# Gate and up biases of the routed experts: loaded once as rows and added by a matmul that picks two of them

## The chip, the cores and the metric

The kernel runs on one core of one Trainium2 chip. The metric is the device time of one execution in microseconds (us). Three runs of the kernel before took 3603.2, 3605.3 and 3605.53 us (median 3605.3 us). All data are fp32.

## The reference

One decoder layer over 256 tokens of width 2048: a token mixer (a diagonal state-space branch and a chunked delta-rule branch, merged by gates), a layer norm, a layer of routed experts, and a second layer norm. The change lies in the routed experts. Each token goes to 4 of 32 experts, and an expert computes, on the tokens that it was given:

```python
gate = jnp.minimum(xb @ w_gate[e] + b_gate[e], SWIGLU_LIMIT)
up = jnp.clip(xb @ w_up[e] + b_up[e], -SWIGLU_LIMIT, SWIGLU_LIMIT)
h = gate * jax.nn.sigmoid(SWIGLU_ALPHA * gate) * (up + 1.0)
return h @ w_down[e] + b_down[e]
```

with `w_gate[e]` and `w_up[e]` of 2048 x 512, `w_down[e]` of 512 x 2048, `b_gate[e]` and `b_up[e]` of 512, and `SWIGLU_LIMIT` 7. The results are summed per token with the router's weights (`b_down` is added elsewhere, by one matmul with the weights of all experts).

## The kernel before

The program is written by hand per engine, with semaphores; the order on each engine is the order of the code. SyncE (SP) issues all DMAs. The phases run one after the other: the projections and the two branches, the gating, the output projection, a layer norm, the router, the routed experts (from about 2547 us to 3571 us in the profiled execution), and the last layer norm.

The experts run as 16 pairs (`PAIRS`), each expert with room for 64 tokens (`CAP`), so that a pair fills 128 partitions or 128 columns: partitions 0 to 63 of a bank belong to the first expert of the pair and 64 to 127 to the second. Where an expert had more than 64 tokens, a flag sends all engines into another branch (`over > 0`), which this input doesn't take. Per pair `i`, TensorE (PE) does, in `sparse(i)`:

- `sgate(i)` (through `expand`, the matmuls of L860): 32 calls of `mm` into bank 0, alternately for the left and the right expert, each with 64 columns of the array and 512 moving columns; each call is two MATMUL records in the profile.
- `sup(i)` (L860 too): the same into bank 1. Gate and up together are the 128 records of L860 in a pair.
- `gather(i + 1)` (L849): selects the tokens of the next pair by a matmul with a 0/1 matrix `Psel`.
- `scatter(i - 1, 0, 6)` and `(6, 8)` (L907; 8 calls, 16 records): spreads the results of the pair before back over the tokens. Between them `turn_hidden` (L876), behind them `turn_weights` (L881), both transposes.
- `sdown(i)` (L891): the down projection, 64 records, again with 64 columns of the array each.

`mm` with start=True begins a sum in a bank, and the later calls add to it. The full array (128 columns) is used in L849, L876, L881 and L907, half columns in L860 and L891.

VectorE (DVE) does `select(i)` (L1592: builds `Psel`, four instructions), `stake_gate(i)` (L1600: reads bank 0, adds the bias tile `pbrow[:, 0]`; L1602: the minimum), `stake_up(i)` (L1608: reads bank 1, adds `pbrow[:, 1]`; L1611: the weights `Pw` for the scatter; L1616: minimum and maximum; L1618, L1621: the products) and `add_scatter` (L1629: adds a bank to the sum of the layer). ScalarE (ACT) copies banks to the tiles that PE reads next (L1119, L1127, L1129, L1137) and does the sigmoid (L1123).

The weights pass through six buffers (`unit`), each of 2 MB: 12 loads per pair (four quarters each of gate, up and down), issued by `reload_unit` (L350), which waits until PE has read the buffer (`unit_read`). The biases of a pair are loaded by `load_biases(i)` (L361): four DMAs, each of which reads one row of 512 numbers and writes it to 64 partitions. From pair 1 on they stand between the second and the third load of weights, behind a wait on `brow_free`, which `stake_up(i - 1)` sets when it has read the bias tile. `stake_gate(i)` waits for them.

The tile `masks` has 8 x 128 columns. Columns 128 to 1023 hold masks of the delta-rule branch and later a copy of state inputs; the experts don't use them. `ident` is a 128 x 128 identity.

Of the kernel before, what the change touches and what calls it, by code (L numbers as in the profile page):

```python
# [67 lines left out]
def build(nc, x, w_in, conv_w, a_log, dt_bias, norm_w, w_dn, lam_re, lam_im, log_dt, b_re, b_im, c_re, c_im,  # L68
# [3 lines left out]
    with ExitStack() as ctx:  # L72
# [138 lines left out]
        ysb = at(4096, D)  # L211
        pbrow = at(6144, 2, F_E)
        Psel = at(TM + 768, MT, 2, CAP)
# [53 lines left out]
        unit_read = [sem(f"unit{i}_free") for i in range(UNITS)]  # L267
        brow_free = sem("brow_free")
        gate_done, gate_taken, up_done, up_taken = sem("gate_done"), sem("gate_taken"), sem("up_done"), sem("up_taken")
# [17 lines left out]
        def _(sp):  # L287
# [69 lines left out]

            def load_biases(i):
                for o in range(2):
                    for c, b in enumerate((b_gate, b_up)):  # L360
                        sp.dma_start(pbrow[CAP * o:CAP * o + CAP, c],  # L361
                                     b[ds(2 * i + o, 1)].rearrange("o n -> (o n)").partition_broadcast(CAP)).then_inc(brow_loaded, 16)

# [28 lines left out]
            load_unit(UNITS - 1, 0)  # L392
            load_biases(0)
            sp.dma_start(ln2row[:, 0], ln2_g.partition_broadcast(P)).then_inc(ln2_loaded, 16)
# [3 lines left out]
            with sp.If(over < 1):  # L398
                for j in range(UNITS, PER_PAIR):
                    reload_unit(j, 0)  # L400
                with sp.Fori(1, PAIRS) as i:
                    for j in range(PER_PAIR):
                        if j == 2:
                            sp.wait_ge(brow_free, i)
                            load_biases(i)
                        reload_unit(j, i)
            with sp.If(over > 0):
                for j in range(UNITS):
                    sp.wait_ge(unit_loaded[j], 16)
                sp.wait_ge(brow_loaded, 64)  # L410
                load_gate(0)
                load_up(0)
                with sp.Fori(0, N_E - 1) as e:
                    sp.wait_ge(gate_done, e + 1)
                    sp.sem_inc(load_free, 1)
                    load_gate(e + 1)
                    sp.wait_ge(dn_taken[1], 4 * e + 1)
                    sp.sem_inc(load_free, 1)
                    load_down(e)
                    sp.wait_ge(up_taken, 2 * e + 2)  # L420
                    sp.sem_inc(load_free, 1)
                    load_up(e + 1)
                sp.wait_ge(dn_taken[1], 4 * N_E - 3)
                load_down(N_E - 1)
# [95 lines left out]
        def _(pe):  # L520
# [332 lines left out]
            def expand(bank, first, i):  # L853
                for q in range(4):
                    j = first + q
                    pe.wait_ge(unit_loaded[j % UNITS], 32 * i + 16 * (j // UNITS) + 16)
                    w = unit[j % UNITS].rearrange("p o (k n) -> p o k n", k=4)
                    for k in range(4):
                        for o in range(2):
                            last = mm(ps[bank][CAP * o:CAP * o + CAP, :], xg[:, 4 * q + k, CAP * o:CAP * o + CAP], w[:, o, k],  # L860
                                      start=q == 0 and k == 0, stop=q == 3 and k == 3)
                    last.then_inc(unit_read[j % UNITS], 1)

            def sgate(i):
                pe.wait_ge(xg_taken, 4 * i + 4)
                if not isinstance(i, int) or i > 1:
                    pe.wait_ge(sc_taken, 8 * i - 8)
                expand(0, 0, i)

# [298 lines left out]
        def _(dve):  # L1168
# [383 lines left out]
            def take_gate(e):  # L1552
                dve.wait_ge(gate_done, e + 1)
                dve.wait_ge(brow_loaded, 32 * e + 96)
                for m in range(MT):
# [33 lines left out]
            def select(i):  # L1589
                for m in range(MT):  # L1590
                    for o in range(2):
                        V.tensor_scalar(Psel[:, m, o], slots1, column(pos, m, i, o), column(sel, m, i, o),  # L1592
                                        ALU.is_equal, ALU.mult)
                dve.drain()  # L1594
                dve.sem_inc(p_built, 1)

            def stake_gate(i):
                dve.wait_ge(unit_read[3], 2 * i + 1)
                dve.wait_ge(brow_loaded, 64 * i + 64)
                V.tensor_tensor(sgb, ps[0][:, :], pbrow[:, 0], ALU.add)  # L1600
                dve.drain()
                V.tensor_scalar(sgb, sgb, LIMIT, None, ALU.min)  # L1602
                dve.drain()
                dve.sem_inc(gate_taken, 1)

            def stake_up(i):
                dve.wait_ge(unit_read[1], 2 * i + 2)
                V.tensor_tensor(shb, ps[1][:, :], pbrow[:, 1], ALU.add)  # L1608
                for m in range(MT):
# [4 lines left out]
                dve.sem_inc(up_taken, 1)  # L1614
                dve.sem_inc(brow_free, 1)
                V.tensor_scalar(shb, shb, LIMIT, -LIMIT, ALU.min, ALU.max)  # L1616
                dve.drain()
                V.scalar_tensor_tensor(out=shb, in0=shb, scalar=1.0, in1=sgb, op0=ALU.add, op1=ALU.mult)  # L1618
# [67 lines left out]
```

## Time and profile before

| what | value |
|---|---|
| median of three runs | 3605.3 us (3603.2 to 3605.53) |
| the profiled execution | 3604.39 us, of which span 3602.3 us |
| PE busy | 3206.1 us, 89% of the span |
| PE weight loads | 2437.7 us, 68% (they overlap the matmuls) |
| DVE busy | 1047.1 us, 29% |
| ACT busy | 482.2 us, 13% |
| DMA moved | 660.87 MB, mean 183 GB/s |
| chain of waits, share of the span | PE 60%, issue 16%, DVE 9%, DVE's sequencer 5%, DMA 3% |

All times of the trace count from the span's start. PE's matmuls are pipelined, their ends are modelled, and a record's duration (592 ns for 512 moving columns at full clock) is longer than the distance from one to the next: distances between starts, or the length of a whole run of records, tell what a matmul costs. In the chain of waits each piece ends where the next begins.

### The profile page before, as it was taken

How to read it: one execution, taken by the hardware profiler on the slowest of the kernel's cores; microseconds unless marked ns; L12 is line 12 of the kernel's file. 1: busy time of each engine (PE TensorE's matmuls, PEld its weight loads, DVE VectorE, ACT ScalarE, POOL GpSimd, SP SyncE). 2: the span in 40 equal slices, each digit the busy share in tenths (PEclk: the TensorE clock that was granted, in tenths of full speed). 3: DMA queues.
4: the chain of work that ended last, by engine and by line, in shares of the span. 5: the costliest groups of instructions: out<-in, count | busy, mean ns of one | idle time of the engine just before them, and what ended most of it. 6: DMA issues, size and time to landing. Idle time of an engine off the chain costs nothing.

```text
span 3602.3 us, 44020 instructions
## 1 busy us (share of the span) xinstructions
PE 3206.1 (89%) x17395; PEld 2437.7 (68%) x17395; DVE 1047.1 (29%) x2650; ACT 482.2 (13%) x632; POOL 106.8 (3%) x189
## 2 busy tenths in 40 slices
PE   6999999999997868787788787895899999999996
PEld 6988888888886757676676676685545445454542
DVE  1433433433423026465570000003111111121114
ACT  1121121121121021101100000000011101111111
POOL 1010010010010000000000000000000000000000
PEclk9999999999999888798898998897899999999998
DMA  5232232242230622232223334273499999999995
GB/s 148 71 116 93 70 116 70 80 130 70 70 116 9 178 94 94 68 99 83 80 94 117 97 113 140 87 275 117 192 406 410 396 409 396 410 409 396 409 396 212
DMA packets 325973, 660.87 MB, mean 183 GB/s; under 512 B 41840, under 2 KB 271344, under 8 KB 275440
## 3 DMA queue, kind: packets, MB, share of 16 engines
q1 hardware_dynamic: 325904, 659.85, 49.9%
q8 instruction: 56, 0.92, 0.1%
q14 instruction: 13, 0.11, 0.0%
HBM read 657.73 MB, written 2.10 MB: 183 GB/s over the span
## 4 chain that ended last, share of the span: by engine, by line
PE 60%; issue 16%; DVE 9%; DVEq 5%; DMA 3%; ACT 2%; SPq 1%; ACTq 1%; POOL 1%; POOLq 1%
PE bank L553 17%; PE bank L860 12%; PE bank L849 6%; PE bank L891 6%; PE bank L907 3%; PE bank L618 3%; PE bank L616 3%; PE bank L762 2%; DVE arena L1401 2%; DVE arena L1403 2%; PE bank L609 2%; DVEq L1400 2%; DMA arena<-in_w_glu_a_dram 2%; PE bank L734 1%; PE bank L703 1%
## 5 line engine op out<-in xcount | busy, mean ns | idle before, releaser
L553 PE MATMUL bank<-arena 128*128 128x256 f32 x5632 | 1285.1, 387 | 117.3 <-DMA arena<-in_w_glu_a_dram 71.0
L553 PEld LDWEIGHTS bank<-arena 128*128 128x128 f32 x5632 | 1081.0, 195 | 274.3 <-issue 90.4
L860 PE MATMUL bank<-arena 128*64 128x512 f32 x2048 | 442.2, 592 | 0.7 <-ACT arena L1119 0.7
L860 PEld LDWEIGHTS bank<-arena 128*64 128x64 f32 x2048 | 147.1, 137 | 292.5 <-issue 290.5
L721 PE MATMUL bank<-arena 128*128 128x256 f32 x1024 | 229.1, 387 | 19.9 <-DMA arena<-in_w_dn_out_dram 19.9
L849 PEld LDWEIGHTS bank<-arena 128*128 128x128 f32 x1024 | 224.8, 311 | 15.4 <-issue 12.2
L721 PEld LDWEIGHTS bank<-arena 128*128 128x128 f32 x1024 | 198.8, 195 | 49.5 <-DMA arena<-in_w_dn_out_dram 16.0
L849 PE MATMUL bank<-arena 128*128 128x128 f32 x1024 | 227.8, 384 | 3.1 <-DVEq L1594 3.1
L891 PE MATMUL bank<-arena 128*64 128x512 f32 x1024 | 223.3, 594 | 7.7 <-ACT arena L1129 7.7
L891 PEld LDWEIGHTS bank<-arena 128*64 128x64 f32 x1024 | 72.2, 137 | 148.4 <-issue 137.0
L1629 DVE TENSOR_TENSOR arena<-arena,bank 128x512 f32<-128x512 f32 x128 | 87.7, 687 | 198.6 <-PE bank L907 198.5
L1600 DVE TENSOR_TENSOR arena<-bank,arena 128x512 f32<-128x512 f32 x16 | 11.1, 692 | 458.6 <-PE bank L860 458.6
L609 PE MATMUL bank<-arena 128*128 128x128 f32 x896 | 123.9, 281 | 7.8 <-DVEq L1253 3.9
L762 PE MATMUL bank<-arena 128*128 128x256 f32 x512 | 115.4, 390 | 12.6 <-DMA arena<-in_w_mix_out_dram 12.6
L609 PEld LDWEIGHTS bank<-arena 128*128 128x128 f32 x896 | 112.4, 191 | 21.0 <-DVEq L1266 13.1
L1435 DVE TENSOR_TENSOR arena<-arena,bank 128x512 f32<-128x512 f32 x8 | 5.5, 689 | 413.9 <-ACTq L1086 413.9
L762 PEld LDWEIGHTS bank<-arena 128*128 128x128 f32 x512 | 100.3, 196 | 27.7 <-issue 13.3
L618 PE MATMUL bank<-arena 128*128 128x128 f32 x896 | 118.3, 275 | 0.0
L616 PE MATMUL bank<-arena 128*128 128x128 f32 x896 | 118.2, 275 | 0.0
L907 PE MATMUL bank<-arena 128*128 128x512 f32 x256 | 115.2, 593 | 2.5 <-DVEq L1613 1.8
L1262 DVE TENSOR_TENSOR arena<-arena,bank 128x512 f32<-128x512 f32 x112 | 77.1, 688 | 137.7 <-PE bank L618 137.7
L616 PEld LDWEIGHTS bank<-arena 128*128 128x128 f32 x896 | 113.3, 192 | 2.9
(277 smaller groups left out, 2264.7 us busy)
## 6 DMA issues: line engine op xcount, KB each, us to landing
arena<-in_w_in_dram SPq DMA_DIRECT2D x72, 2048.0 KB, 8.4
arena<-in_w_gate_dram SPq DMA_DIRECT2D x64, 2048.0 KB, 16.3
arena<-in_w_up_dram SPq DMA_DIRECT2D x64, 2048.0 KB, 13.3
arena<-in_w_down_dram SPq DMA_DIRECT2D x64, 2048.0 KB, 19.2
arena<-in_w_dn_out_dram SPq DMA_DIRECT2D x16, 2048.0 KB, 11.3
arena<-in_w_glu_a_dram SPq DMA_DIRECT2D x8, 2048.0 KB, 8.3
arena<-in_w_glu_b_dram SPq DMA_DIRECT2D x8, 2048.0 KB, 13.7
arena<-in_w_mix_out_dram SPq DMA_DIRECT2D x8, 2048.0 KB, 11.1
```

What stands on the lines that cost most here:

```text
L553: last = mm(ps[bank][:, ct * T:ct * T + T], ring[:, buf, k, ct * P:ct * P + P], rhs[:, k, :], start=k == 0, stop=k == KD - 1)
L609: last = mm(ps[3 + 2 * c][:, a * P:a * P + P], At[:, c, a], Ti[:, c, a], start=True, stop=True)
L616: mm(ps[3 + 2 * c][:, a * P:a * P + P], Tt[:, c, a], Pm[:, c, a], start=True, stop=True)
L618: last = mm(ps[4 + 2 * c][:, a * P:a * P + P], Pm[:, c, a], Tt[:, c, a], start=True, stop=True)
L721: last = mm(ps[1][:, ct * T:ct * T + T], ring[:, buf, k, ct * P:ct * P + P], oT[:, half * KD + k, :], start=half == 0 and ct == 0 and k == ...
L762: last = mm(ps[bank][:, m * SC:m * SC + SC], mg[:, k, m * P:m * P + P], ring[:, buf, k, :], start=k == 0, stop=k == KD - 1)
L849: last = mm(ps[4 + b][:, k * P:k * P + P], h1[:, m, 4 * b + k::KD], Psel[:, m].rearrange("p o c -> p (o c)"), start=m == 0, stop=m == MT - 1)
L860: last = mm(ps[bank][CAP * o:CAP * o + CAP, :], xg[:, 4 * q + k, CAP * o:CAP * o + CAP], w[:, o, k], start=q == 0 and k == 0, stop=q == 3 ...
L891: last = mm(ps[4 + n][CAP * o:CAP * o + CAP, :], shT[:, k, CAP * o:CAP * o + CAP], unit[j % UNITS][:, o, n * 512:n * 512 + 512], start=k = ...
L907: last = mm(ps[(2, 3, 0, 1)[n % 4]][:, :], pwT[:, (n // 4) * P:(n // 4) * P + P], ysb[:, (n % 4) * 512:(n % 4) * 512 + 512], start=True, s ...
L1262: V.tensor_tensor(Ti[:, c], Ti[:, c], ps[3 + 2 * c][:, :].rearrange("p (a t) -> p a t", a=GV), ALU.subtract)
L1629: V.tensor_tensor(av, av, ps[(2, 3, 0, 1)[n % 4]][:, :], ALU.add).then_inc(sc_taken, 1)
```

## The change

The two bias arrays (32 experts x 512 numbers each) are loaded once, as they are: expert `e` on partition `e`, gate in `bias_gu[:, 0]`, up in `bias_gu[:, 1]`. `select(i)` builds beside `Psel` a 32 x 128 matrix `pair_pick`: column `c` of the left half has its one on row `2i`, of the right half on row `2i + 1`. At the head of `sgate(i)` two matmuls with `pair_pick` stationary and the bias rows moving (32 rows, all 128 columns of the array, 512 moving columns) begin the sums in banks 0 and 1 with the biases on every partition; the matmuls of `expand` then all add. The four DMAs per pair, the wait on `brow_free` and DVE's waits for the biases go. On DVE the addition of the bias goes out of L1600 and L1608, and what stood behind each of them (minimum; minimum and maximum) reads the bank directly, so that L1602 and L1616 go; one copy into `pair_pick` is added in `select`.

```diff
-        pbrow = at(6144, 2, F_E)
+        bias_gu = at(6144, 2, F_E)
+        pair_pick = masks[0:N_E, P:2 * P]
...
-            def load_biases(i):
-                for o in range(2):
-                    for c, b in enumerate((b_gate, b_up)):
-                        sp.dma_start(pbrow[CAP * o:CAP * o + CAP, c],
-                                     b[ds(2 * i + o, 1)].rearrange("o n -> (o n)").partition_broadcast(CAP)).then_inc(brow_loaded, 16)
+            def load_biases():
+                for c, b in enumerate((b_gate, b_up)):
+                    sp.dma_start(bias_gu[0:N_E, c], b).then_inc(brow_loaded, 16)
...
-            load_biases(0)
+            load_biases()
...
                     for j in range(PER_PAIR):
-                        if j == 2:
-                            sp.wait_ge(brow_free, i)
-                            load_biases(i)
                         reload_unit(j, i)
...
                             last = mm(ps[bank][CAP * o:CAP * o + CAP, :], xg[:, 4 * q + k, CAP * o:CAP * o + CAP], w[:, o, k],
-                                      start=q == 0 and k == 0, stop=q == 3 and k == 3)
+                                      start=False, stop=q == 3 and k == 3, skip_group_check=True)
...
             def sgate(i):
                 pe.wait_ge(xg_taken, 4 * i + 4)
+                if isinstance(i, int) and i == 0:
+                    pe.wait_ge(brow_loaded, 32)
                 if not isinstance(i, int) or i > 1:
                     pe.wait_ge(sc_taken, 8 * i - 8)
+                for c in range(2):
+                    mm(ps[c][:, :], pair_pick, bias_gu[0:N_E, c], start=True, stop=False, skip_group_check=True)
                 expand(0, 0, i)
...
+                V.tensor_copy(pair_pick.rearrange("p (o c) -> p o c", o=2),
+                              ident[0:N_E, ds(2 * i, 2)].unsqueeze(2).to_broadcast([N_E, 2, CAP]))
                 dve.drain()
                 dve.sem_inc(p_built, 1)
 
             def stake_gate(i):
                 dve.wait_ge(unit_read[3], 2 * i + 1)
-                dve.wait_ge(brow_loaded, 64 * i + 64)
-                V.tensor_tensor(sgb, ps[0][:, :], pbrow[:, 0], ALU.add)
-                dve.drain()
-                V.tensor_scalar(sgb, sgb, LIMIT, None, ALU.min)
+                V.tensor_scalar(sgb, ps[0][:, :], LIMIT, None, ALU.min)
                 dve.drain()
                 dve.sem_inc(gate_taken, 1)
 
             def stake_up(i):
                 dve.wait_ge(unit_read[1], 2 * i + 2)
-                V.tensor_tensor(shb, ps[1][:, :], pbrow[:, 1], ALU.add)
+                V.tensor_scalar(shb, ps[1][:, :], LIMIT, -LIMIT, ALU.min, ALU.max)
...
                 dve.sem_inc(up_taken, 1)
-                dve.sem_inc(brow_free, 1)
-                V.tensor_scalar(shb, shb, LIMIT, -LIMIT, ALU.min, ALU.max)
-                dve.drain()
```

PE in the loop over pairs 1 to 14, from the head of the loop to the first quarter of the gate weights, before (`xg_taken`: the gathered tokens are copied; `sc_taken`: the banks of an earlier scatter are read):

```order
L931 UNCONDITIONAL_BRANCH
L931 ISA
L867 ISA [waits xg_taken]
L856 ISA [waits sc_taken]
L860 MATMUL bank0<-arena 64x512 [waits unit0_loaded]
L860 MATMUL bank0<-arena 64x512 x7
```

and now:

```order
L930 UNCONDITIONAL_BRANCH
L930 ISA
L864 ISA [waits xg_taken]
L866 MATMUL bank0<-arena,masks 128x512 [waits sc_taken]
L866 MATMUL bank1<-arena,masks 128x512
L851 ISA
L855 MATMUL bank0<-arena 64x512 [waits unit0_loaded]
L855 MATMUL bank0<-arena 64x512 x7
```

Two matmuls on the whole array stand between `sdown` of the pair before and the first gate matmul; the waits are those of before. In pair 0 the first of the two also waits for the biases.

SP in the same loop, around the second and third load of weights, before:

```order
L350 ISA [waits unit1_free]
L350 DMA arena<-in_w_gate_dram 128x2x2048
L361 ISA [waits brow_free]
L361 DMA arena<-in_b_gate_dram 64x512
L361 DMA arena<-in_b_up_dram 64x512
L361 ISA
L361 DMA arena<-in_b_gate_dram 64x512
L361 DMA arena<-in_b_up_dram 64x512
L350 ISA [waits unit2_free]
L350 DMA arena<-in_w_gate_dram 128x2x2048
```

and now:

```order
L350 ISA [waits unit1_free]
L350 DMA arena<-in_w_gate_dram 128x2x2048
L350 ISA [waits unit2_free]
L350 DMA arena<-in_w_gate_dram 128x2x2048
```

The four bias DMAs and their wait are gone; the waits of the weights stand as before. DVE in pair 0 and before pair 1, before:

```order
L1592 TENSOR_SCALAR arena<-arena 128x64 x4
L1600 TENSOR_TENSOR arena<-bank0,arena 128x512 [waits brow_loaded,unit3_free]
L1602 TENSOR_SCALAR arena<-arena 128x512
L1592 TENSOR_SCALAR arena<-arena 128x64 x4
L1608 TENSOR_TENSOR arena<-bank1,arena 128x512 [waits unit1_free]
L1611 TENSOR_SCALAR arena<-arena 128x64 x4
L1616 TENSOR_SCALAR arena<-arena 128x512
L1618 SCALAR_TENSOR_TENSOR arena<-arena 128x512
```

and now:

```order
L1591 TENSOR_SCALAR arena<-arena 128x64 x4
L1593 COPY masks<-ident 32x128
L1600 TENSOR_SCALAR arena<-bank0 128x512 [waits unit3_free]
L1591 TENSOR_SCALAR arena<-arena 128x64 x4
L1593 COPY masks<-ident 32x128
L1606 TENSOR_SCALAR arena<-bank1 128x512 [waits unit1_free]
L1609 TENSOR_SCALAR arena<-arena 128x64 x4
L1613 SCALAR_TENSOR_TENSOR arena<-arena 128x512
```

The copy stands behind the four instructions of `select`, ahead of the signal that `gather` waits for; two instructions over 512 columns are gone.

## Rows read from the trace of the kernel before

**Rows 1.** Windows of the expert stage: length, busy us per engine (records), PEclk, DMA share, GB/s.

```profile
2748.04:2811.65 63.61, 63.15 (x281) 31.39 (x278) 10.99 (x22) 7.55 (x12) 0.00 (x0) 1.00 0.99 404
...
3511.30:3538.80 27.50, 27.49 (x130) 8.96 (x124) 1.12 (x2) 1.21 (x2) 0.00 (x0) 1.00 1.01 422
```

**Rows 2.** The chain that ended last, one pair and the next pair's start: start, length.

```profile
2748.04 27.47 PE bank L860 x128
2775.51 14.17 PE bank L849 x64
2789.68 5.15 PE bank L907 x12
...
2797.69 13.95 PE bank L891 x64
2811.65 27.47 PE bank L860 x128
```

**Rows 3.** Waits, 2700 to 3603 us: engine, line, releaser, total us, times, longest.

```profile
PE bank L891 <- ACT arena L1129: 6.5, 14, 0.5
...
PEld bank L860 <- DMA arena<-in_w_up_dram: 0.6, 2, 0.3
```

**Rows 4.** Waits of SP's queue in the same stretch.

```profile
SPq L355 <- PE bank L891: 375.1, 52, 20.4
SPq L355 <- PE bank L860: 300.6, 106, 2.9
...
SPq L361 <- DVEq L1614: 15.0, 13, 1.2
```

**Rows 5.** DMA issues of the whole span: count, size of each, us from issue to landing.

```profile
arena<-in_w_gate_dram SPq DMA_DIRECT2D x64, 2048.0 KB, 16.3
...
arena<-in_b_gate_dram SPq DMA_DIRECT2D x32, 128.0 KB, 23.2
arena<-in_b_up_dram SPq DMA_DIRECT2D x32, 128.0 KB, 22.3
```

**Rows 6.** The window of the 8 calls of L795, columns as in rows 1.

```profile
2523.00:2537.30 14.30, 14.02 (x16) 5.14 (x16) 0.21 (x1) 0.00 (x0) 0.00 (x0) 0.50 0.00 0
```

**Rows 7.** Two weight loads of L795 on the timeline, five records apart: start, length.

```profile
2525.13 0.33 PEld L795 LDWEIGHTS bank<-arena 32*128 32x128 f32 x1 [0.52 <-issue]
...
2529.40 0.33 PEld L795 LDWEIGHTS bank<-arena 32*128 32x128 f32 x1 [0.52 <-issue]
```

**Rows 8.** PE groups: line, array part, moving data, count, busy us, mean ns, idle before.

```profile
L849 PE MATMUL bank<-arena 128*128 128x128 f32 x1024 | 227.8, 384 | 3.1 <-DVEq L1594 3.1
...
L907 PE MATMUL bank<-arena 128*128 128x512 f32 x256 | 115.2, 593 | 2.5 <-DVEq L1613 1.8 <-ACT arena L1137 0.7
```

**Rows 9.** PE timeline where the part of the array in use changes: start, length, records.

```profile
1596.87 0.81 PE L721 MATMUL bank<-arena 128*128 128x256 f32 x3
...
1597.61 0.34 PE L703 MATMUL bank<-masks,arena 32*128 32x64 f32 x4
...
2711.30 0.60 PE L860 MATMUL bank<-arena 128*64 128x512 f32 x2
...
2711.83 0.48 PE L849 MATMUL bank<-arena 128*128 128x128 f32 x1
...
2734.09 0.65 PE L891 MATMUL bank<-arena 128*64 128x512 f32 x2 [0.46 <-ACT arena L1129]
```

**Rows 10.** DVE timeline: a small copy from a bank, and the first `select`.

```profile
2522.80 0.41 DVE L1531 COPY arena<-bank 32x256 f32<-32x256 f32 x1 [0.73 <-PE bank L790]
...
2546.64 0.98 DVE L1592 TENSOR_SCALAR arena<-arena 128x64 f32<-128x64 f32 x4 [1.43 <-issue]
```

**Rows 11.** The chain that ended last, behind the up matmuls of the last pair.

```profile
3538.84 0.69 DVE arena L1608
3539.53 0.94 DVEq L1613
```

More of the change, by code:

```diff
@@ L267, in build @@
         unit_read = [sem(f"unit{i}_free") for i in range(UNITS)]
-        brow_free = sem("brow_free")
         gate_done, gate_taken, up_done, up_taken = sem("gate_done"), sem("gate_taken"), sem("up_done"), sem("up_taken")
@@ L409, in _ @@
                     sp.wait_ge(unit_loaded[j], 16)
-                sp.wait_ge(brow_loaded, 64)
+                sp.wait_ge(brow_loaded, 32)
                 load_gate(0)
@@ L1553, in take_gate @@
                 dve.wait_ge(gate_done, e + 1)
-                dve.wait_ge(brow_loaded, 32 * e + 96)
+                dve.wait_ge(brow_loaded, 32 * e + 64)
                 for m in range(MT):
```

## The prediction

> **What bounds the kernel now.** I read the windows over the expert stage first, since all that the change touches lies there. In a pair's period of 63.61 us PE is busy for 63.15, its clock is granted at 1.00 (2.4 GHz), and the DMA share is 0.99 at 404 GB/s [rows 1]. Two resources look full at once, so the waits decide which one sets the pace. The chain of waits runs through PE without a break: 27.47 us of gate and up, 14.17 of gather, 5.15 and 1.72 of scatter, 13.95 of down projection, and the next pair starts 63.61 us behind the last [rows 2]. PE waits once per pair, for ACT's copy of the transposed hidden values, 6.5 us in 14 times, and its weight loads waited for weights 0.6 us in all [rows 3]. SP's queue waits 375.1 + 300.6 = 675.7 of 903 us for PE to free a buffer [rows 4]. So PE is the bound, and the transfers follow it. DVE is busy for 10.99 of 63.61 us and has no part in the period, save at the two ends (first `select`, last pair).
>
> How near is DMA? A pair moves 12 x 2.10 MB of weights and 4 x 0.131 MB of biases [rows 5], together 25.69 MB, which in 63.61 us is the 404 GB/s of the window. In the last window the rate is 422 GB/s [rows 1]; at that rate a pair would need 60.9 us. DMA is 2.7 us per pair from being the bound, and its share near 1 shows transfers in flight all the time, not a limit.
>
> **The change part by part.**
>
> *The two bias matmuls, on PE, which is the path.* A matmul call with 512 moving columns is two records. The nearest by shape are the scatter's, whole array: 12 records in 5.15 us, 0.429 us each, at full clock [rows 2]. They have 128 rows under them, the bias calls 32. The trace has that case too: L795, 8 calls, 16 records in 14.02 us at a granted clock of 0.50 [rows 6]; its weight loads start (2529.40 - 2525.13) / 5 = 0.854 us apart [rows 7], which is 0.427 us at full clock. So fewer rows make a call no cheaper, and the load of the 32 rows hides behind the matmul before it. Per pair 2 x 2 x 0.429 = 1.72 us; over 16 pairs 27.5 us. Nothing goes from PE: `expand` has the same matmuls, of which the first now adds where it began a sum.
>
> *Two more changes of the part of the array in use.* `sdown` ahead and `expand` behind use half the columns. Until now they adjoined, both with 64 columns; now a block with 32 rows and 128 columns stands between. From L860 to L849 (halves to whole) the last two records start at 2711.30 and the next one at 2711.83, 0.53 us where 27.47 / 64 = 0.43 is the rhythm, and that first record takes 0.48 where the mean of its group is 0.38: 0.20 us in all [rows 2, 8, 9]. From L721 (whole) to L703 (32 rows) the rhythm is (0.81 - 0.38) / 2 = 0.215 us, the last record starts at 1597.30 and the next at 1597.61, 0.09 us late [rows 9]. For the way back to halves there is only L891, which begins after a wait: its first record takes 0.65 where L860's takes 0.60, so 0.05 of load in the open [rows 9], and with the 0.10 of the change 0.15 us. I take 0.15 for each way, 0.30 per pair, 4.8 us over 16. Ends: nothing, if such short loads hide (27.5 alone); and 0.43 each, if the tail of a record (0.59 - 0.43 = 0.16), a whole weight load (0.33 at half clock, 0.17) and the 0.10 all stand in the open: 13.8 us.
>
> The Trainium skill (TensorEngine Tiling (Array Packing), Key Properties) says that going to another tiling mode drains TensorE, while another tile of the same mode doesn't. The late starts above agree, 0.09 to 0.10 us each. By that rule the term of 4.8 us stands; without it the change would cost the 27.5 us of the calls alone.
>
> *DVE.* Per pair two instructions over 512 columns go, and the reads of the two banks change from an addition to a minimum (or minimum and maximum) at the same size. All of it lies beside PE, and PE's only wait in the loop is for ACT behind its own transposes: 0. In the last pair PE does wait for DVE, for the read of bank 1 and the four small instructions behind it, 0.69 + 0.94 us [rows 11]. Both stay ahead of the signal, so 0; at best the read costs as little as one from SBUF, a gain under 0.4 us. The copy into `pair_pick` lies ahead of the first gather, where PE waits 3.1 us for DVE [rows 8, 10]. Its price is between one of the four small instructions (0.98 / 4 = 0.25 us) and a copy of 32 x 256 from a bank (0.41 us) [rows 10]: 0.3 us, once. In the loop it lies some 10 us ahead of its use.
>
> *DMA and SP.* 64 DMAs of 128 KB (8.4 MB) become two of 64 KB. What hides them now is PE's 63.61 us per pair, so what is saved is hidden as well: 0. In `load_biases` SP waited 15.0 us in 13 times behind DVE [rows 4]; the next buffer is only free once PE is well into the down projection, so this delayed no load. Pair 0 now has a wait on PE for the biases. They are issued with the last loads ahead of the router, some 60 us before their use, and landed in 23 us when they were four times as large [rows 5]: 0. Less traffic at the router may let its data land sooner, by at most 0.39 MB / 404 GB/s = 1.0 us; they are issued ahead of the biases, so I take 0.
>
> The sum: 27.5 + 4.8 + 0.3 = 32.6 us. On the profiled execution (3604.4 us, of which 2.1 lie around the span) this gives 3637.0; the median is 0.9 above that execution, hence 3638 us.
>
> **The rivals.**
>
> *DMA sets the pace, and the change is faster.* For it: a share of 0.99 in the expert stage, and loads that take 16 us where the stage needs one every 5.3. Were PE merely following the transfers, 0.52 of 25.69 MB less per pair would give back 2.0% of 63.61, 1.3 us, and PE's new work would lie in the slack: 3605.3 - 16 x 1.3 = 3585 us. It decides once PE's period is below what the bytes need, 60.9 us at 422 GB/s; with the change PE needs 65.6 us and the bytes 25.17 / 422 = 59.6. Against it: those figures, PE's 0.6 us of waiting for weights, and a period that doesn't vary by 0.01 us.
>
> *The calls alone.* The changes of array part are hidden: 3605.3 + 27.8 = 3633 us. For it: the load of 32 rows is short. Against it: rows 9, three places of three.
>
> *The changes cost all that they can:* 27.5 + 13.8 + 0.3 gives 3647 us. Against it: no place in rows 9 costs over 0.20.
>
> *A quarter of the array at a quarter of the price, no change that can be told.* The calls use 32 of 128 rows. If such a call took a quarter of the time, 16 x 1.72 / 4 = 6.9 us, 3612 us. Against it: L795's rhythm, and both calls need the same 32 rows, so neither can run beside the other.
>
> The Trainium skill (TensorEngine Tiling (Array Packing), Theoretical Speedup) gives up to four times for a dimension of 32 or less, by tiles that run side by side. With that rule one comes to this rival's time. It needs calls on different rows, and here there is one block of rows.
>
> **How the numbers follow.** A measurement of this kernel tells about 0.2% (7.2 us) from no change. Forecast, the sum within 3 us: 0.80. The calls alone: 0.10. All that the changes can cost: 0.05. DMA's pace: 0.03, the only case that is faster. A quarter of the price: 0.02, the only one within 0.2%. Slower is the rest, 0.95. The range goes from just below the calls alone to 5 us above the forecast, 3632 to 3643 us, and leaves out the last three cases and a little of the first.
>
> **What would show it.** In the profile after: the period of a pair at 65.6 us, uniform; ahead of the gate matmuls in each pair four records of the new line, 0.43 us apart, together near 2.0 us with what surrounds them; PE still without waits for DMA; a window of a pair near 25.17 / 65.6 = 384 GB/s, and SP's waits for PE longer; DVE's groups over 512 columns without the two that went, and no gain from it. The forecast is wrong if the period stays at 63.6 or falls (DMA, or cheap calls), if it comes to 65.3 (the changes are hidden) or above 66 (they cost more), or if PE waits somewhere in the loop where it did not.

## The result, and the profile after

| | before | after |
|---|---|---|
| median (range) | 3605.14 us (3603.2 to 3605.53, 4 runs) | 3635.72 us (3634.4 to 3638.77, 4 runs) |
| profiled execution, span | 3602.3 us | 3632.7 us |
| period of a pair, pairs 2 to 14 | 63.61 us | 65.67 us |
| first gather starts, after the span's start | 2547.71 us | 2545.22 us |
| DMA moved | 660.87 MB | 652.61 MB |

The change made the kernel slower: ratio 1.0087, interval 1.0075 to 1.0099, or 31 us. Forecast were 3638 us and 3632 to 3643. The median lies 2.3 us under the forecast and 2.7 above the 3633 us of the rival "the calls alone", so it does not tell the two apart; the period of a pair does.

The windows of one pair and the chain of waits through it, in the kernel after (columns as in rows 1 and 2; L855 is L860 of before, L844 is L849, L906 is L907, L890 is L891, and L866 holds the bias matmuls):

```profile
2753.49:2819.16 65.67, 65.21 (x285) 31.97 (x286) 10.27 (x21) 7.55 (x13) 0.00 (x0) 1.00 0.93 384
```

```profile
2751.58 1.91 PE bank L866 x4
2753.49 27.62 PE bank L855 x128
2781.11 14.17 PE bank L844 x64
2795.28 5.15 PE bank L906 x12
...
2803.29 13.95 PE bank L890 x64
2817.25 1.91 PE bank L866 x4
2819.16 27.62 PE bank L855 x128
```

Against [rows 2] one block, the four records of L866, is new (1.91 us) and one is longer (27.62 where 27.47 stood); gather, scatter and down projection are the same to the hundredth. 1.91 + 0.15 = 2.06 us in 15 pairs; in pair 0, where the block stands behind the gather and a wait and not behind a down projection, the interval between gathers grows by 1.91 (44.46 where 42.55 stood). Together that is 32.8 us. The rate is 384 GB/s, as forecast; the DMA share fell from 0.99 [rows 1] to 0.93.

How the 1.91 and the 0.15 come about shows on PE's timeline around one block (start, length, records):

```profile
2619.22 1.03 PE L890 MATMUL bank<-arena 128*64 128x512 f32 x4
2620.18 0.69 PE L866 MATMUL bank<-arena,masks 32*128 32x512 f32 x1
...
2620.71 1.45 PE L866 MATMUL bank<-arena,masks 32*128 32x512 f32 x3
...
2622.09 0.65 PE L855 MATMUL bank<-arena 128*64 128x512 f32 x2
```

The last two records of L890 start at 2619.65 (1.03 - 0.60 behind 2619.22), the first of L866 at 2620.18: 0.53 us where the rhythm (from one start to the next) is 0.43, and it takes 0.69 where the others take 0.59. That is 0.10 + 0.10 on the way in. On the way back the last record of L866 starts at 2621.57, the first two of L855 at 2622.09, 0.52 us, and take 0.65 instead of 0.60: 0.09 + 0.05. Together 0.34 us beside the 4 x 0.429 of the records.

Waits of PE and of SP's queue from 2700 us on:

```profile
PE bank L890 <- ACT arena L1128: 6.5, 14, 0.5
```

```profile
SPq L355 <- PE bank L890: 440.0, 52, 25.3
SPq L355 <- PE bank L855: 332.8, 107, 4.9
```

PE waits as before [rows 3], and nowhere for the biases or the weights. SP waits 440.0 + 332.8 = 772.8 us for PE, 97 more than in [rows 4]: the transfers have more time, not less. DVE in pair 0:

```profile
2544.03 0.98 DVE L1591 TENSOR_SCALAR arena<-arena 128x64 f32<-128x64 f32 x4 [1.41 <-issue]
2544.93 0.21 DVE L1593 COPY masks<-ident 32x128 f32<-32x128 f32 x1
2576.06 0.69 DVE L1600 TENSOR_SCALAR arena<-bank 128x512 f32<-128x512 f32 x1 [30.93 <-PE bank L855]
```

The read of a bank with a minimum takes the 0.69 us that the read with an addition took; the copy takes 0.21. The first gather starts 1.19 us behind the start of `select` (2545.22 - 2544.03), where it was 1.07 (2547.71 - 2546.64) [rows 10]: on the path the copy costs 0.12 us.

From the first gather to the end of the span it is 1054.6 us before and 1087.4 after: 32.8 us more, those of the pairs. In both profiled executions the granted clock is 1.00 from within the first gather (2551.4 and 2549.4 us) to the end of the last scatter. The 2.5 us by which the first gather starts earlier come from stages that the change doesn't touch. In the other profiles of this study it starts between 2541.8 and 2548.2 us, so this difference says nothing of the change.

### The profile page after: what moved, and what is told of

Same layout as the page of the kernel before. It is cut to its first block, busy times and chain, and to the rows that moved or that the text cites. A ratio compares the mean times of both kernels' runs of the same rounds, so it can differ in the third digit from the quotient of the medians.

```text
span 3632.7 us, 43945 instructions
## 1 busy us (share of the span) xinstructions
PE 3238.9 (89%) x17459; PEld 2447.3 (67%) x17459; DVE 1034.3 (28%) x2634; ACT 482.2 (13%) x632; POOL 106.8 (3%) x189
## 2 busy tenths in 40 slices
DMA packets 320949, 652.61 MB, mean 180 GB/s; under 512 B 40848, under 2 KB 270352, under 8 KB 270416
## 4 chain that ended last, share of the span: by engine, by line
PE 61%; issue 15%; DVE 9%; DVEq 5%; DMA 3%; ACT 2%; SPq 1%; ACTq 1%; POOL 1%; POOLq 1%
PE bank L548 17%; PE bank L855 12%; PE bank L844 6%; PE bank L890 6%; PE bank L906 3%; PE bank L613 3%; PE bank L611 3%; PE bank L757 2%; DVE arena L1400 2%; DVE arena L1402 2%; PE bank L604 2%; DVEq L1399 2%; DMA arena<-in_w_glu_a_dram 2%; PE bank L729 1%; PE bank L698 1%
## 5 line engine op out<-in xcount | busy, mean ns | idle before, releaser
L855 PE MATMUL bank<-arena 128*64 128x512 f32 x2048 | 443.0, 593 | 0.0
L855 PEld LDWEIGHTS bank<-arena 128*64 128x64 f32 x2048 | 145.6, 137 | 295.4 <-issue 295.4
L844 PEld LDWEIGHTS bank<-arena 128*128 128x128 f32 x1024 | 224.8, 311 | 15.5 <-issue 12.2
L844 PE MATMUL bank<-arena 128*128 128x128 f32 x1024 | 227.8, 384 | 3.2 <-DVEq L1595 3.2
L890 PE MATMUL bank<-arena 128*64 128x512 f32 x1024 | 223.3, 594 | 7.7 <-ACT arena L1128 7.7
L890 PEld LDWEIGHTS bank<-arena 128*64 128x64 f32 x1024 | 72.1, 137 | 148.5 <-issue 137.0
L1600 DVE TENSOR_SCALAR arena<-bank 128x512 f32<-128x512 f32 x16 | 11.1, 692 | 490.6 <-PE bank L855 490.6
L906 PE MATMUL bank<-arena 128*128 128x512 f32 x256 | 115.2, 593 | 2.5 <-DVEq L1611 1.8
```

Of the source, the lines that this page charges most:

```text
L844: last = mm(ps[4 + b][:, k * P:k * P + P], h1[:, m, 4 * b + k::KD], Psel[:, m].rearrange("p o c -> p (o c)"), start=m == 0, stop=m == MT - 1)
L890: last = mm(ps[4 + n][CAP * o:CAP * o + CAP, :], shT[:, k, CAP * o:CAP * o + CAP], unit[j % UNITS][:, o, n * 512:n * 512 + 512], start=k = ...
L906: last = mm(ps[(2, 3, 0, 1)[n % 4]][:, :], pwT[:, (n // 4) * P:(n // 4) * P + P], ysb[:, (n % 4) * 512:(n % 4) * 512 + 512], start=True, s ...
```

## The experiments

Ratios are to the kernel before, run on the same chip in the same job; its median there was 3602.3 us for e1 to e8 and 3604.0 for e9 to e12. Periods are distances between the starts of successive gathers (L844 in the kernel after). Rows are from the chain of waits unless said otherwise.

**e1: no bias matmuls.**

```diff
-                for c in range(2):
-                    mm(ps[c][:, :], pair_pick, bias_gu[0:N_E, c], start=True, stop=False, skip_group_check=True)
...
-                                      start=False, stop=q == 3 and k == 3, skip_group_check=True)
+                                      start=q == 0 and k == 0, stop=q == 3 and k == 3)
```

> The changed kernel without the two bias matmuls per pair, so gate and up biases are left out of the result; transfers, waits and DVE are those of the change. Theory (PE's own work sets the pace, and the 2.06 us per pair are the calls and what surrounds them): pair period back at 63.6 us, total within 2 us of the kernel before, about 3605 us. Rival (DMA held the pace and the lighter traffic gives something back, which the matmuls merely outweigh): 16 x 1.3 = 21 us faster than before, about 3584 us. Rival 2 (part of the loss is in SP, DVE or the new copy, not in the calls): more than 3608 us.

3602.91 us, ratio 1.0002 (0.9992 to 1.0012); period 63.61 us. The gate and up matmuls (L855) adjoin the down projection (L888) again:

```profile
3047.23 13.95 PE bank L888 x64
3061.18 9.01 PE bank L855 x41
```

(The view ends within L855.) All else that the change does, fewer transfers, waits and DVE instructions, is worth nothing here and costs nothing. The loss is the calls.

**e2: bias matmuls over a quarter of the columns.**

```diff
-                    mm(ps[c][:, :], pair_pick, bias_gu[0:N_E, c], start=True, ...
+                    mm(ps[c][:, 0:P], pair_pick, bias_gu[0:N_E, c, 0:P], start=True, ...
```

> The changed kernel with bias matmuls over 128 of the 512 columns; the biases of the other 384 columns are left out. Theory (each block of calls costs its columns plus a fixed 0.34 us for the two changes of array part): 4 records at 0.107 to 0.12 us plus 0.34, 0.77 to 0.82 us per pair, 12 to 13 us over the kernel before, about 3618 us. Rival (no fixed cost, the block's 2.06 us scale with its columns): 2.06 / 4 = 0.52 us per pair, 8 us, about 3613 us.

3613.67 us, ratio 1.0029 (1.0018 to 1.0041); period 64.39 us, 0.78 more than before.

```profile
3008.37 0.64 PE bank L866 x4
3009.01 27.62 PE bank L855 x128
```

0.64 + 0.15: a quarter of the columns costs 38% of the full price. The 0.15 behind the block is that of the full calls. The fixed part is there; a block that scaled with its columns would have cost 0.52. From the first gather to the end the profiled execution is 12.5 us longer than before, as the theory has it; the medians differ by 11.4.

**e3: each call twice.**

```diff
+                for c in range(2):
+                    mm(ps[c][:, :], pair_pick, bias_gu[0:N_E, c], start=True, stop=False, skip_group_check=True)
```

> The changed kernel with each bias matmul issued twice (the second overwrites the same bank with the same values). Theory: no further change of array part, so only 4 more records of 0.429 us per pair, 1.72 us, 27.5 us over the changed kernel, about 3663 us; pair period 67.4 us. Rival (every call has a share of the surrounding cost): 2.06 us per pair more, 33 us, about 3669 us; period 67.7.

3688.05 us, ratio 1.0238 (1.0221 to 1.0255), 86 us, where 58 and 64 follow from the two expectations. Of the 13 periods from the third interval between gathers on, four have the 67.39 us of the theory, seven 69.0 and two 70.7:

```profile
2763.54 1.91 PE bank L866 x4
2765.45 1.72 PE bank L868 x4
2767.17 27.62 PE bank L855 x128
...
2830.93 1.91 PE bank L866 x4
2832.84 2.04 PE bank L868 x4
```

and the windows over the same two blocks (columns as in rows 1):

```profile
2763.54:2767.17 3.63, 3.63 (x11) 1.41 (x12) 0.00 (x0) 1.87 (x2) 0.00 (x0) 1.00 1.02 431
2830.93:2837.50 6.57, 6.57 (x16) 2.17 (x18) 0.00 (x0) 1.87 (x2) 0.00 (x0) 0.74 1.02 430
```

The second four calls cost 1.72 us without anything around them, so the price per call and the price per block are apart as forecast. But PE's clock falls: in the second window 0.74 is granted on the mean, the level of 1.2 GHz for part of it, though PE was busy all the time. Such a fall costs 1.64 or 3.34 us. Neither theory had it. It came 2.5 to 3.9 us behind the start of the eight records, in the last third of them or just behind, in 11 of the 16 pairs; e9 and e10 are made for it.

**e4: the same array part as the neighbours.**

```diff
+            g.memset(bias_gu[32:64], 0.0)
+            g.memset(bias_gu[64:P], 0.0)
+            g.memset(masks[32:64, P:2 * P], 0.0)
+            g.memset(masks[64:P, P:2 * P], 0.0)
...
                 for c in range(2):
-                    mm(ps[c][:, :], pair_pick, bias_gu[0:N_E, c], start=True, ...
+                    for o in range(2):
+                        mm(ps[c][CAP * o:CAP * o + CAP, :], pick_all[:, CAP * o:CAP * o + CAP], bias_gu[:, c], start=True, ...
```

> The changed kernel with the bias matmuls in the array part of their neighbours: 128 rows (rows 32 to 127 of both operands are zeros, written once by GpSimd), 64 columns for each expert of the pair, 8 records per pair of which two run side by side. Theory: the columns cost the same (1.72 us per pair), the two changes of array part vanish, 0.34 us per pair less: 5.4 us under the changed kernel, about 3630 us; pair period 65.3 us, and no late start around the calls. Rival (the late starts come from starting a sum in a bank or from the new operands, not from the array part): same as the changed kernel, 3636 us.

3629.23 us, ratio 1.0075 (1.0058 to 1.0092); period 65.33 us.

```profile
3011.59 1.72 PE bank L877 x8
3013.30 27.47 PE bank L864 x128
```

1.72 exactly, and the gate and up matmuls (L864 here) are back at 27.47. The 0.34 us are the two changes of array part, in rows and columns at once (the rows in use and the half columns were not changed one by one). The period shows the 0.34; the ratios alone (1.0075 and 1.0087, from two jobs) overlap.

**e5: the calls in PE's wait.**

```diff
                 turn_weights(i)
+                if more:
+                    for c in range(2):
+                        if not first:
+                            pe.wait_ge(sc_taken, 8 * i + c - 1)
+                        begin_bias(c)
                 sdown(i)
```

> The changed kernel with the bias matmuls of pair i + 1 moved from the head of sgate to the place behind turn_weights of pair i, where PE waits about 0.7 us for ACT's copy anyway; each waits for DVE to have read its bank. Theory: the calls take 1.72 us of which some 0.6 to 0.7 fall into that wait, and the array part changes there in any case, so the period is 63.6 + 1.2 = 64.8 us: 18 to 19 us over the kernel before, about 3624 us. Rival (PE's own work counts wherever it stands, or the second call waits for DVE's read so long that nothing is won): 3633 to 3636 us.

3625.51 us, ratio 1.0059 (1.0042 to 1.0076); period 64.99 us.

```profile
3065.35 0.22 PE bank L884 x2
3065.57 1.91 PE bank L860 x4
3067.48 2.72 PE bank L894 x11
```

The 0.42 us in which the chain ran through ACT are gone, and the block has its 1.91 us: 1.38 us per pair where 1.2 were expected. I had taken the wait for 0.6 to 0.7; in the chain it is 0.42. The blocks, 1.91 us in pair 0 and 15 times 1.38, are 22.6 us; the medians differ by 23.2, so the price of the blocks explains what the total has above the 18 to 19 us of the theory.

The profiled execution, the slowest of the four, has more. The first interval between gathers is 47.80 us (42.55 before) and the second 64.02 (57.96): beyond the blocks 3.3 and 4.7 us, in which the clock fell. The windows of the block of pair 0, and of the two transposes ahead of the moved block of pair 1:

```profile
2556.95:2560.52 3.57, 3.57 (x6) 1.03 (x8) 0.00 (x0) 1.25 (x1) 0.00 (x0) 0.54 0.00 0
2604.74:2606.13 1.39, 1.39 (x6) 1.06 (x7) 0.00 (x0) 0.32 (x1) 0.00 (x0) 0.59 1.00 418
```

The moved place began neither fall. The first came 0.25 us into a block that stands where the kernel after has it; the second 1.1 us ahead of the moved block, behind a wait of PE of 0.66 us. Kernels without any such block have a fall there too: in e7, e8 and e11 the clock fell behind this gather, around the start of the down projection. In e7 and e11 the second interval is 1.6 and 1.7 us longer for it; that it is 4.7 here may be the block's doing, which no run separates.

**e6: three bf16 pieces.**

```diff
+            g.tensor_copy(pieces[0:N_E], full)
+            g.tensor_tensor(rest, full, pieces[0:N_E], ALU.subtract)
+            g.tensor_copy(pieces[32:64], rest)
...
+                        mm(ps[c][CAP * o:CAP * o + CAP, :], pick3[0:96, CAP * o:CAP * o + CAP], bias3[0:96, c], start=True, ...
```

> The changed kernel with the fp32 bias rows split once, by GpSimd, into three bf16 pieces that sum to them (96 rows), the picking matrix in bf16 too, and calls on 64 columns for each expert: 4 records of one pass per pair, two side by side. Theory (a call's price is passes times columns): 2 x 0.216 us per pair = 0.43, without changes of array part, 7 us, with two more copies ahead of the first gather 0.4: about 3613 us; period 64.0 us. Rival (mixing fp32 and bf16 calls on PE costs something of its own, of the size of an array change): 0.8 us per pair, 3618 us or more.

3610.67 us, ratio 1.0019 (1.0009 to 1.0028); period 64.05 us.

```profile
3005.76 0.43 PE bank L887 x4
3006.20 27.47 PE bank L875 x128
```

A call in bf16 is one record where fp32 has two, and two records side by side take 0.215 us where in e4 they took 0.43; the four take 0.43 us. No extra cost between the types shows.

**e7 and e8: bias transfers two and five times, in the kernel before.**

```diff
                             load_biases(i)
+                            load_spare(i)
```

`load_spare` holds the same four loads, once (e7) or four times (e8), into space that nothing reads.

> The kernel before with each bias load issued twice, the second into spare space. Theory (DMA has slack: 26.2 MB at 422 GB/s need 62.1 us of 63.6): no change, 3605 us within 2; SP waits for PE correspondingly less. Rival (DMA holds the pace): 0.52 MB more, 1.3 us per pair, 3625 us.

> The kernel before with each bias load issued five times, four of them into spare space: 27.8 MB per pair, which at 422 GB/s need 65.9 us. Theory (DMA becomes the bound beyond 63.6 us): period about 65.9 us, PE waits for weights, 3605 + 15 x 2.2 = 3638 us. Rival (the 422 GB/s is no ceiling, or small broadcasts cost other than their bytes): no change if the ceiling lies higher; above 3645 us if broadcasts cost more than their bytes, or SP's 20 issues per pair delay the weights.

e7: 3650.35 us, ratio 1.0132 (1.0115 to 1.0149). e8: 3773.24 us, 1.0451 (1.0413 to 1.0489). Both far above the theory, and e7 above its rival too; e8 is where its rival put it, above 3645 us. In e7 (L869 is L860 of before):

```profile
2748.03 6.89 PE bank L869 x32
...
2755.09 18.70 DMA arena<-in_w_up_dram
...
2773.84 3.65 PE bank L869 x16
```

and its waits from 2700 us on:

```profile
PEld bank L869 <- DMA arena<-in_w_up_dram: 71.3, 40, 2.2
...
PE bank L869 <- DMA arena<-in_w_up_dram: 36.6, 37, 1.3
```

A load of weights, issued when PE frees the buffer, now lands after PE wants it, 18.70 us later. The period is 65.60 us at first and 67.3 at the end of the loop; in e8 it is 72.8 and later 76.4. DMA had far less slack than the 2.7 us that I took from the 422 GB/s of one window. In e7 SP's issues are no part of it: its queue still waits 340.2 + 277.6 = 617.8 us for PE, and around 2790 us the last of the eight bias loads of a pair leaves 13 us before the next load of weights. In e8 they may be: SP's wait for the buffers of the down projection shrinks from 277.6 to 60.5 us, and PE waits 51.4 us for gate weights as well.

**e11: the same bytes in one plain transfer.**

```diff
+                            sp.dma_start(spare, w_gate[ds(2 * i, 1)].rearrange("o (p k) n -> p (o k n)", k=KD)[:, 0:1024]).then_inc(brow_loaded, 16)
```

> The kernel before with 0.52 MB more per pair, as e7 loads, but as one transfer of 4 KB pieces from the weights into spare space where e7 adds four broadcasts of one row to 64 partitions. e7 came out 48 us slower where its bytes at 422 GB/s said no change. Theory (a broadcast of a row costs about twice its bytes; the bytes alone fit the slack, or nearly): period 63.6 to 64.4 us, at most 12 us slower. Rival (the slack was used up by bytes of any shape, DMA stood at its limit): period near 65 to 66 us, 25 us slower or more, as e7.

3616.44 us, ratio 1.0047 (1.0029 to 1.0065); period 65.3 us in six pairs, then 64.0 to 64.8. The waits for weights, as in e7, are 28.5 and 11.4 us:

```profile
PEld bank L862 <- DMA arena<-in_w_up_dram: 28.5, 23, 2.2
PE bank L862 <- DMA arena<-in_w_up_dram: 11.4, 14, 1.3
```

Between the two expectations, so both held in part. Half a megabyte more of either shape does not fit. In the first loop periods the four broadcasts and the plain transfer cost nearly the same (65.6 and 65.25 us); they part later, at 67.3 against 64.5 us, and the medians are 48 and 12 us above the kernel before.

The packets in the traces tell the early price. A packet of 8 KB of weights takes one DMA engine 0.316 us on the mean (kernel before), one of 2 KB of the broadcasts 0.13 to 0.14 (kernel before, e7), one of 4 KB of the plain transfer 0.23 to 0.26 (e11). Over 16 engines the four broadcasts of a pair, 256 packets, are then 2.1 to 2.3 us and the plain transfer, 128 packets, 1.8 to 2.1, where the same bytes in packets of 8 KB would be 1.3. The weights of a pair, 3072 packets, are 60.7 us. What parts the two later is not in the packets: between 3300 and 3500 us e7 has a DMA share of 0.98 and e11 of 1.01.

**e9: e4 with each call twice.** The edit is e4's block of calls, written twice.

> e4 (bias calls on 128 rows of which 96 hold zeros, half columns) with every call issued twice, 16 records in a row. e3 had the same columns in a row on 32 rows, and its granted clock fell to half for 3.4 or 6.8 us behind such a stretch in nearly every second pair. Theory (a stretch of 3.4 us on 32 of 128 rows is what made the clock fall): no fall in the expert stage, period 63.61 + 2 x 1.72 = 67.05 us throughout, 55 us over the kernel before, about 3658 us. Rival (the number of calls, or operands that are mostly zeros, make it fall): periods of 68.7 and more in part of the pairs, 3670 us or more.

3657.39 us, ratio 1.0152 (1.0137 to 1.0168); period 67.04 us in all pairs. The window over most of the stage, in e9 and then in e3:

```profile
2700.00:3500.00 800.00, 794.46 (x3508) 388.90 (x3506) 123.14 (x252) 90.75 (x144) 0.00 (x0) 1.00 0.91 375
```

```profile
2700.00:3500.00 800.00, 794.92 (x3342) 385.77 (x3339) 118.79 (x246) 86.16 (x137) 0.00 (x0) 0.98 0.89 370
```

Same moving columns, same banks, the same ones in the picking matrix. On 128 rows, 96 of them zeros, the clock stays; on 32 rows it falls. The two kernels also differ in the records (16 with 64 columns of the array against 8 with 128) and in the changes of array part.

**e10: two blocks apart.**

```diff
+                for c in range(2):
+                    mm(ps[4][:, :], ident[0:N_E, :], bias_gu[0:N_E, c], start=True, stop=True, skip_group_check=True)
                 for k in range(KF):
                     j = 8 + k
```

> The changed kernel with a second block of two such calls (32 rows, 128 columns, results overwritten) at the head of sdown, 14 us of half-column matmuls away from the first. As many 32-row records per pair as in e3, but never more than 1.7 us of them in a row. Theory (only a long stretch on few rows makes the clock fall): no fall, period 65.67 + 1.72 + 0.1 to 0.2 = 67.5 us throughout, 62 us over the kernel before, about 3665 us. Rival (the total of 32-row work in a pair counts): falls as in e3, 3680 us or more.

3676.42 us, ratio 1.0202 (1.0187 to 1.0218). From the third interval on the period is 67.58 us eight times, as the theory has it, and 69.28 five times; that only a long stretch makes the clock fall is refuted. The down projection (L892) behind the second block, in a pair without and one with a fall:

```profile
2677.40 1.98 PE bank L886 x4
2679.38 13.88 PE bank L892 x64
...
2744.98 1.98 PE bank L886 x4
2746.96 15.58 PE bank L892 x64
```

```profile
2744.98:2750.50 5.52, 5.52 (x14) 1.83 (x16) 0.04 (x1) 0.00 (x0) 0.00 (x0) 0.69 0.00 0
```

Four records on 32 rows were enough here, right behind PE's wait for ACT, though not each time. The same four records between two stretches of full work, 15 times in the kernel after and 15 times here, made no fall.

In pair 0 even the block at the head of `sgate` stands behind a wait, of 0.66 us. Its first 5.8 us in e10 and in the kernel after:

```profile
2560.28:2566.10 5.82, 5.82 (x16) 1.83 (x18) 0.00 (x0) 1.25 (x1) 0.00 (x0) 0.71 0.00 0
```

```profile
2560.15:2566.00 5.85, 5.85 (x24) 2.03 (x26) 0.00 (x0) 1.25 (x1) 0.00 (x0) 1.00 0.00 0
```

Up to there both kernels run the same instructions. So the kernel after has a place where the clock can fall, and did not in the one execution that was profiled.

**e12: the kernel before, with an earlier down projection.**

```diff
-                pe.wait_ge(htr_taken, 2 * i + 2)
+                pe.wait_ge(htr_taken, 2 * i + 1)
...
-                    for n in range(4):
+                    for n in (0, 2, 3, 1) if k == 0 else range(4):
+                        if k == 0 and n == 1:
+                            pe.wait_ge(htr_taken, 2 * i + 2)
```

> The kernel before with sdown starting when the transposed hidden values are copied, not when ACT has also copied the transposed scatter weights: its first quarter goes through banks 4, 6, 7 and then 5, and only bank 5 waits for that second copy. PE's wait of 0.73 us from the last transpose to the first down matmul then goes but for a change of array part. Theory: 0.5 to 0.6 us less per pair, period 63.0 to 63.1 us, 8 to 10 us faster than before, about 3594 us. Rival (DMA stands at its limit, e7): the period stays at 63.3 or more and PE waits for weights instead, under 5 us faster.

3597.49 us (3591.07 to 3604.31, 11 runs), ratio 0.9981 (0.9972 to 0.9990): 7 us faster than the kernel before. The period is 63.08 us, 0.53 less, as the theory has it; from the first gather to the end the profiled execution is 8.0 us shorter.

```profile
2725.90 1.72 PE bank L909 x4
2727.62 0.22 PE bank L881 x2
2727.84 13.88 PE bank L893 x64
2741.72 27.47 PE bank L860 x128
```

```profile
PEld bank L860 <- DMA arena<-in_w_up_dram: 1.7, 3, 0.9
```

The down projection follows the transposes without a gap. From 2700 us on the weights are late three times, so DMA keeps up with 25.69 MB in 63.08 us, 407 GB/s. In e11, 26.22 MB at 407 GB/s would take 64.4 us, which is its later period. So before the change DMA needed no more than 63.1 of 63.61 us. Whether it could do with less, no run here shows.

## Why the prediction was right, and where it was not

**PE sets the pace: right.** e1 takes all transfers and DVE instructions of the change away from the kernel before and moves nothing.

**27.5 us for the calls: right.** The second set of calls in e3 costs 1.72 us per pair, e4 1.72, e9 twice that. That 32 rows are no cheaper than 128, read from L795 at half clock [rows 6, 7], holds at full clock: 0.429 us per record. The rival of a quarter of the price falls with this.

**4.8 us for the changes of array part: right in kind, a little small.** It is 0.34 us per pair, 5.3 in all (0.19 in pair 0, which has no way in from halves): 0.20 on the way in, which is what [rows 9] show for halves to whole, and 0.14 on the way back. I had lowered the first to 0.15. e2 shows the part as fixed, e4 makes it vanish. The rivals "the calls alone" and "all that they can cost" fall with this. The rule of the Trainium skill (TensorEngine Tiling (Array Packing), Key Properties) that a change of tiling mode drains TensorE, and a change of tile within a mode doesn't, agrees: of the 0.34 us some 0.19 are late starts (0.10 and 0.09), and in e4, in the mode of the neighbours, there are none.

**0.3 us for the copy, 0 for DVE, DMA and the wait on the biases: right in kind.** The copy takes 0.21 us, of which 0.12 are on the path.

**The sum** was 32.6 us, of which 32.3 lie behind the first gather; there it took 32.8 more. The medians differ by 30.6 (ratio: 31); the rest lies in the stages ahead, in which executions differ by more than that. That the median came within 2.3 us of the forecast is in part luck: what confirms the mechanism is the period, forecast at 65.6 us and measured at 65.67.

**DMA's slack: wrong, without a share in the sum.** The step that failed is "at that rate a pair would need 60.9 us": the window of 422 GB/s in [rows 1] has no transfers of biases, and a pair of the kernel before also has 256 packets of 2 KB, which take longer for their bytes. The prediction also set the DMA share aside ("transfers in flight all the time, not a limit"). It was the better measure: 0.99 of 63.61 us is 63.0 us of work for the DMA engines, and 60.7 + 2.1 us by the packets (e11) is nearly the same. e12 shows that a slack of 0.5 us was there (63.08 us, share 1.00); e11, e7 and e8, with more to move, all have longer periods. So the slack was some 0.5 to 0.8 us and not 2.7. The rival in which DMA sets the pace was nearer than 3 in 100 suggests. It is refuted by e1 all the same: at 63.61 us per pair PE was still the later of the two. The 2.7 would have misled anyone who wanted to shorten PE's part.

**The clock: not in the prediction.** It did not fall during the pairs in the profiled execution of the kernel after. That was not certain: with one more such block per pair (e3, e10) it falls in the loop, and in pair 0 it fell at the very block that the kernel after has there (e10, e5). A fall costs 1.6 us or more each time, against a forecast range of 11 us.

## What to carry to other kernels

Work that is moved from engines and queues with idle time to the engine that sets the pace costs its full price, here 2.06 us per pair for two small matmuls, and what it frees elsewhere is worth nothing. Here a matmul's price was its moving columns times its records (two in fp32, one in bf16), whether it used 32, 96 or 128 rows; keep its array part that of its neighbours (zeros in the other rows do), and split exact small operands into bf16 pieces if they must go through PE. Take the limit of the transfers from their share over a whole period and from the sizes of their packets, or from an experiment that adds to them, and not from the best window.

## What the runs showed of the hardware

- The granted clock of a TensorE that is busy without a gap can fall to 1.2 GHz. In e3 it did near the end of eight fp32 records of 512 columns on 32 of 128 rows, in e10 at four of them that followed a wait of some 0.5 us (5 of 13 times in the loop); in e9, with the same columns on 128 rows of which 96 were zeros, it did not. Rows in use are not all of it: in the kernel before, L795 (32 rows, busy for 14.02 of 14.30 us) stayed at 0.50 from end to end [rows 6], but so did L784 ahead of it (128 rows, 32 moving columns, busy for 13.83 of 14.00). What exactly decides was not tried: rows in use, part of the array, weights loaded on few rows, or several of them.
- Packets of 2 KB cost more than their bytes: 0.13 to 0.14 us of a DMA engine against 0.316 for 8 KB, 1.7 to 1.8 times as much per byte (kernel before, e7). Twelve more broadcasts of one 2 KB row to 64 partitions per pair (e8 against e7) lengthen the first loop periods from 65.6 to 72.9 us, 0.6 us for each; their 64 packets of 0.14 us over 16 engines are 0.57, where 128 KB at 407 GB/s would be 0.32. Why the periods of e7 and e8 grow along the loop, while those of e11 don't, stays open.
- A change of the array's part costs 0.20 us from halves to 32 rows of the whole width and 0.14 back, beside the calls themselves (the kernel after, e2, e4).
